# Prompt attention of a hybrid decoder layer: triangular sums in two fp32r passes instead of one fp32 product

## The reference

```
z = einsum('bqhd,bkhd->bhqk', q, k) * HEAD_DIM ** -0.5 + bias
mask = kpos[None, :] < qpos[:, None]
log_1m = where(mask, log_sigmoid(-z), 0.0)
between = cumsum(log_1m, axis=3, reverse=True) - log_1m
weights = exp(where(mask, log_sigmoid(z) + between, -inf))
out = einsum('bhqk,bkhd->bqhd', weights, v)
```

## Time and profile before

| | |
|---|---|
| median of 3 runs | 2051.55 us |
| the profiled execution | 2058.1 us, its span 2056.5 us |
| TensorE busy in the span | 1851.8 us (90%), 13899 matmuls |
| VectorE, ScalarE, GpSimd busy | 820.1, 614.7, 397.1 us |
| prompt attention | from 392.2 to 510.9 us of the span |
| decode, linear attention, RWKV | behind it, to about 1100 us |
| output projection and MLP | the rest |

### The profile page before, as it was taken

One profiled execution on the slowest core, in us unless ns is written; L12 is line 12 of the kernel. 1 busy time (PEld: TensorE's weight loads), 2 busy tenths in 40 slices (PEclk: granted clock), 3 DMA queues, 4 the chain that ended last, 5 costly groups with the idle time before them and its releaser, 6 DMA issues.

```text
span 2056.5 us, 33982 instructions
## 1 busy us (share of the span) xinstructions
PE 1851.8 (90%) x13899; PEld 1539.0 (75%) x13899; DVE 820.1 (40%) x1286; ACT 614.7 (30%) x1421; POOL 397.1 (19%) x606
## 2 busy tenths in 40 slices
PE   4999999999766798688886996999999999999996
PEld 4999999843435675577784445988888888999995
DVE  7111111265437673533321445333344333433336
ACT  3111111365546555322221222222222222222223
POOL 6400021487353556100010001000000000000004
PEclk9999999999777655697877998999999999999998
DMA  5111121200541011000003201111111111111102
GB/s 152 52 42 40 44 90 55 80 7 2 178 133 35 26 31 28 1 2 1 2 1 124 62 26 51 41 41 41 41 41 54 48 41 41 41 50 52 41 20 87
DMA packets 103829, 100.07 MB, mean 49 GB/s; under 512 B 15522, under 2 KB 89906, under 8 KB 103714
## 3 DMA queue, kind: packets, MB, share of 16 engines
q1 hardware_dynamic: 91266, 81.15, 13.2%
q0 software_dynamic: 6720, 17.11, 2.7%
q10 hardware_dynamic: 5728, 0.19, 0.2%
HBM read 85.78 MB, written 12.65 MB: 48 GB/s over the span
## 4 chain that ended last, share of the span: by engine, by line
PE 51%; DVE 4%; ACT 1%; DMA 1%; issue 1%; POOLq 0%; POOL 0%; SPq 0%; DVEq 0%
PE ps L416 12%; PE ps L417 12%; PE ps L418 12%; PE ps L2407 6%; PE ps L2052 1%; PE ps L1978 1%; DVE arena L2161 1%; DVE arena L2566 1%; PE ps L2073 1%; PE ps L2069 1%; DMA arena<-in_w_out 1%; PE ps L2105 1%; PE ps L2094 1%; PE ps L2125 0%; PE ps L2123 0%
## 5 line engine op out<-in xcount | busy, mean ns | idle before, releaser
L416 PE MATMUL ps<-h_split,w_split 128*128 128x384 f32 (+1 forms) x768 | 251.1, 327 | 3.4 <-DVE w_split L2550 3.4
L418 PE MATMUL ps<-h_split,w_split 128*128 128x384 f32 (+1 forms) x768 | 250.9, 327 | 0.0
L417 PE MATMUL ps<-h_split,w_split 128*128 128x384 f32 (+1 forms) x768 | 250.9, 327 | 0.0
L2577 DVE TENSOR_TENSOR arena<-arena,ps 128x1024 f32<-128x1024 f32 x144 | 175.5, 1219 | 164.3 <-PE ps L418 164.3
L417 PE MATMUL ps<-w_split,u_split 128*128 128x512 f32 (+1 forms) x576 | 224.5, 390 | 0.0
L416 PE MATMUL ps<-w_split,u_split 128*128 128x512 f32 (+1 forms) x576 | 224.4, 390 | 0.0
L418 PE MATMUL ps<-w_split,u_split 128*128 128x512 f32 (+1 forms) x576 | 224.3, 389 | 0.0
L2599 POOL TENSOR_TENSOR arena<-arena 128x1024 f32<-128x1024 f32 (+1 forms) x9 | 23.3, 2594 | 773.7 <-DVE arena L2566 773.7
L2558 DVE TENSOR_TENSOR u_split<-above_u_split,u_split 128x384 fp32r<-128x384 f32 (+1 forms) x96 | 51.5, 537 | 297.2 <-ACT above_u_split L2531 297.1
L2510 ACT ACTIVATE w_split<-below_w_split 128x1024 fp32r<-128x1024 f32 x64 | 64.1, 1048 | 339.1 <-PE ps L418 321.7
L416 PEld LDWEIGHTS ps<-h_split,w_split 128*128 128x128 f32 x768 | 144.7, 188 | 5.1 <-issue 3.6
(11 more groups left out here) (380 smaller groups left out, 3532.4 us busy)
## 6 DMA issues: line engine op xcount, KB each, us to landing
below_w_split<-in_w_up SPq DMA_DIRECT2D x32, 512.0 KB, 4.9
below_w_split<-in_w_down SPq DMA_DIRECT2D x32, 512.0 KB, 3.8
w_raw<-in_w_in SPq DMA_DIRECT2D x27, 512.0 KB, 3.9
arena<-in_x_prompt SPq DMA_DIRECT2D x16, 512.0 KB, 3.7
arena<-in_cache_sb_k SPq DMA_DIRECT2D x64, 128.0 KB, 2.4
arena<-in_cache_sb_v POOLq DMA_DIRECT2D x64, 128.0 KB, 2.6
nat_scratch<-nat_stage POOLq DMA_DIRECT2D x32, 128.0 KB, 2.0
arena<-nat_scratch SPq DMA_DIRECT2D x16, 256.0 KB, 2.7
```

Of the source, the lines that this page charges most:

```text
L416: pe.matmul(out, w_hi, x_hi, start=first, stop=False)
L417: pe.matmul(out, w_hi, x_lo, start=False, stop=False)
L418: return pe.matmul(out, w_lo, x_hi, start=False, stop=last)
L2577: dve.tensor_tensor(y_acc[0:r, i, :], y_acc[0:r, i, :], p, ALU.add).then_inc(S("dn_out"), 1)
```

## The change

The triangular product of `exponents` is done in two fp32r passes over a high and a low part of the softplus. The triangle is copied to an fp32r tile (`sb_tri`) once. For each block ScalarE copies the softplus of both heads to `sb_hi` with rounding to fp32r (`high`), and VectorE subtracts that from the softplus into `sb_lo` (`low`); both tiles have one buffer, so `high(n)` waits for `exponents(n - 1)`. The mask product uses bf16 copies of `ident` and `neg_big`. The sum product stays fp32. VectorE's order becomes low(n + 1), clipped(n + 3), softplus(n + 2); in ScalarE's, high(n + 1) stands between weights(n) and log_sums(n + 2). `exponents` waits for `sb_sum` and `sb_lo` at the head of the products that need them.

```
+        sb_eye, sb_mask = (mixT[:, n, T:TOK].bitcast(BF16) for n in range(2))
...
             def exponents(n):
                 pe.wait_ge(S("sb_sp"), n + 1)
-                if kt < 4 * G + 3:
-                    pe.wait_ge(S("sb_sum"), n)
-                if kt >= 4 * G:
-                    pe.wait_ge(S("sb_spm"), sb_diagonals(n))
                 for c in range(2):
                     bank = ps[:, 2 * (n % 3) + c, 0:w]
                     if kt >= 4 * G:
-                        pe.matmul(bank[:, 0:P], ident, neg_big, start=False, stop=False, skip_group_check=True)
+                        pe.matmul(bank[:, 0:P], sb_eye, sb_mask, start=False, stop=False, skip_group_check=True)
                     if kt < 4 * G + 3:
+                        if c == 0:
+                            pe.wait_ge(S("sb_sum"), n)
                         pe.matmul(bank, neg_ones, sb_sum[:, (n - 1) % 2, c, c0:512], ...)
-                    pe.matmul(bank, neg_tri, sb_sp[:, n % 3, c, 0:w], start=False, stop=True,
-                              skip_group_check=True).then_inc(S("sb_x"), 1)
+                    if c == 0:
+                        pe.wait_ge(S("sb_lo"), n + 1)
+                    pe.matmul(bank, sb_tri[:, :], sb_hi[:, c, 0:w], start=False, stop=False, skip_group_check=True)
+                    pe.matmul(bank, sb_tri[:, :], sb_lo[:, c, 0:w], start=False, stop=True, skip_group_check=True)\
+                        .then_inc(S("sb_x"), 1)
...
+            def low(n):
+                w = sb_geometry(n)[4]
+                dve.wait_ge(S("sb_hi"), n + 1)
+                dve.tensor_tensor(sb_lo[:, :, 0:w], sb_sp[:, n % 3, :, 0:w], sb_hi[:, :, 0:w].bitcast(F32),
+                                  ALU.subtract).then_inc(S("sb_lo"), 1)
+
             clipped(0)
+            dve.tensor_copy(sb_tri[:, :], neg_tri).then_inc(*did("dve"))
+            dve.tensor_copy(sb_eye, ident).then_inc(*did("dve"))
+            dve.tensor_copy(sb_mask, neg_big).then_inc(*did("dve"))
+            dve.wait_ge(*so_far("dve"))
             clipped(1)
+            softplus(dve, 0)
+            clipped(2)
+            softplus(dve, 1)
+            low(0)
             for n in range(SBN):
-                softplus(dve, n)
+                if n + 1 < SBN:
+                    low(n + 1)
+                if n + 3 < SBN:
+                    clipped(n + 3)
                 if n + 2 < SBN:
-                    clipped(n + 2)
+                    softplus(dve, n + 2)
...
             if n >= 3:
-                dve.wait_ge(S("sb_x"), 2 * (n - 2))
                 dve.wait_ge(S("sb_sum"), n - 2)
...
+            def high(n):
+                act.wait_ge(S("sb_sp"), n + 1)
+                if kt >= 4 * G:
+                    act.wait_ge(S("sb_spm"), sb_diagonals(n))
+                if n >= 1:
+                    act.wait_ge(S("sb_x"), 2 * n)
+                act.activation(sb_hi[:, :, 0:w], sb_sp[:, n % 3, :, 0:w], ACT.Copy).then_inc(S("sb_hi"), 1)
+
             log_sums(0)
             log_sums(1)
+            high(0)
             for n in range(SBN):
                 weights(n)
+                if n + 1 < SBN:
+                    high(n + 1)
                 if n + 2 < SBN:
                     log_sums(n + 2)
```

More of the change, by code:

```diff
@@ L572, in build @@
         sb_sum = at(WR + 3072, 2, 2, 512)
+        with ExitStack() as place:
+            place.enter_context(nc.sbuf_tensor("below_sb_hi", [P, CONST_END + 2 * TOK], F32))
+            sb_hi = place.enter_context(nc.sbuf_tensor("sb_hi", [P, 2, 512], F32R))
+            place.enter_context(nc.sbuf_tensor("below_sb_lo", [P, TOK - 1024], F32))
+            sb_lo = place.enter_context(nc.sbuf_tensor("sb_lo", [P, 2, 512], F32R))
+            place.enter_context(nc.sbuf_tensor("below_sb_tri", [P, WR + 5120 - CONST_END - 3 * TOK - 1024], F32))
+            sb_tri = place.enter_context(nc.sbuf_tensor("sb_tri", [P, P], F32R))
+        sb_eye, sb_mask = (mixT[:, n, T:TOK].bitcast(BF16) for n in range(2))
         def sb_geometry(n):
@@ L705, in log_sums @@
                 act.activation(zc, zc, ACT.Ln, bias=one_col).then_inc(S("sb_l"), 1)
+            def high(n):
+                pr, G, kt, q0, w, c0, hg = sb_geometry(n)
+                act.wait_ge(S("sb_sp"), n + 1)
[4 more added lines that the diff above has]
+                act.activation(sb_hi[:, :, 0:w], sb_sp[:, n % 3, :, 0:w], ACT.Copy).then_inc(S("sb_hi"), 1)
             log_sums(0)
             log_sums(1)
+            high(0)
             for n in range(SBN):
                 weights(n)
+                if n + 1 < SBN:
+                    high(n + 1)
                 if n + 2 < SBN:
```

## The result

The changed kernel takes 2079.14 us in the median of 4 runs (2076.9 to 2085.8) beside 2055.47 for the kernel before (4 runs). The ratio is 1.0112, with a 95% interval of 1.0083 to 1.0142: slower by about 23 us. The profiled execution has a span of 2075.9 us.

What follows compares the result with a forecast made beforehand. TensorE's issue bounds the stage before; afterwards the 18.7 us saved stay hidden behind VectorE and GpSimd. The median 2051.6, plus 20.5 for the loop and head and 5 for the clock, gives 2077 us; range 2056 to 2095.

Steps and rivals of the forecast that it cites:

- TensorE's issue was the bound before: In prompt attention before the change, TensorE issues without idle time, so its 5.70 us per full-width block is the period.
- the port: In prompt attention, a VectorE operation with two SBUF inputs waits until GpSimd's current one is over; L674 takes 1.30 median.
- `low` waits out a sum and then needs 1.1 us: In each full block, low waits out GpSimd's 2.36 us sum, then needs 1.1: 3.7 us from softplus to its end.
- E(3): E(n) is the end of exponents(n), where outputs starts; E(3) to E(7) was forecast at 21.5 us against 18.3.
- VectorE goes ahead of GpSimd's next operation: Where GpSimd has its next operation ready, the waiting two-input VectorE operation goes first, as the row at 467.04 shows.
- The periods: From low(n) to low(n+1): 6.4 us in full blocks off the diagonal against 5.70, and 6.8 in 512-wide diagonal ones.
- The head of the stage: Before E(3): low(0) lies behind copies and other VectorE work, +2.8 us, and the three blocks to E(3) lose about 0.9.
- the three copies: At the stage's start, three VectorE copies of 128 columns before low(0): 0.6 us together, at most 1.3.
- The clock: TensorE's waits in the stage lower its clock: two to three falls at about 2 us, +5; upper bound +60.
- The gross saving of 18.7 us: On TensorE in the stage: 13.7 us from the fp32r triangular products and 5.0 from bf16 mask products, if TensorE stays the bound.
- TensorE busy for 95 to 105 us in the stage: A sign to look for in the changed kernel's trace, in a prompt attention stage of about 140 us.
- The rival that `low` does not wait: In the stage, low does not wait for the port: plain period 5.1 us, total 2051, or 2036 if VectorE hides; 8%.

Runs made afterwards that it cites:

- the short shift: The changed kernel with only GpSimd's token-shift operations cut to 72 or fewer columns, sums at full size: 2079.13 us (one run).
- the swapped order: The changed kernel with VectorE's order low(n+1), softplus(n+2), clipped(n+3), so softplus before clipped: 2076.5 us (4 runs), ratio to the kernel before 1.0098.
- GpSimd's operations short: The changed kernel with sums cut to 8 columns per head and token-shift operations to 72 or fewer, waits kept: 2055.35 us (10 runs), ratio 0.9998.

## Why the prediction was right, point by point

- **TensorE's issue was the bound before: right, but for a few diagonal blocks.** The bf16 mask alone shortens the stage, only where masks are, and in eight of twelve diagonal blocks by the whole saving. In three blocks TensorE already waited for the port, 1.3 us together.
- **`low` waits out a sum and then needs 1.1 us: right, and nearly the whole cause.** It ends 1.08 behind the sum in each plain block, and with no long operation on GpSimd 21.2 of the 22.8 us are gone; the head keeps 3.9 of its 5.6, against a gain of 2.3 behind E(3).
- **VectorE goes ahead of GpSimd's next operation: right**, though it rested on one row; a shift behind a sum now lasts 2.5 to 3.4 us in each block where `low` falls into the sum, against 2.0 to 2.4 before. The Trainium skill, "SBUF — State Buffer", section "Summary: rules for kernel authors", says that with two SBUF inputs on VectorE and a GpSimd operation that reads SBUF, the second one to issue is blocked fully until the first finishes. The trace agrees: `low` ends 1.08 us behind the sum, about what its 1024 columns take by themselves (1.23 us for the whole operation with the port free).
- **The periods: right within 3% by group, in part by luck.** Plain 6.2 against 6.4. Group by group, forecast and measured: E(3) to E(7) 21.5 and 21.7, E(7) to E(11) 24.8 and 24.3, E(11) to E(23) 67.3 and 68.0. Single diagonal blocks miss by more and in both directions: those 384 wide were forecast at 6.0 and took 6.68, 7.55 and 5.28, those 512 wide at 7.2 and took 6.64, 5.94 and 7.73. The forecast periods hold no loss of clock and the measured ones do, as the point on the clock shows.
- **The head of the stage: too cheap.** From first scores to E(3) I forecast 3.7 more; it is 25.5 against 19.9, 5.6 more. The step that failed is the three copies "0.6 together, at most 1.3": they took 1.7. The first two waited for GpSimd's clearing, 393.14 to 394.96, as VectorE's and GpSimd's timelines of the changed kernel show:

```profile
393.50 1.54 DVE L669 CAST sb_tri<-arena 128x128 fp32r<-128x128 f32 x1
393.63 1.48 DVE L670 CAST arena<-arena 128x128 bf16<-128x128 f32 x1
395.03 0.21 DVE L671 CAST arena<-arena 128x128 bf16<-128x128 f32 x1
```

```profile
393.14 1.82 POOL L762 MEMSET arena<- 128x2048 f32 x1
```

 The rest of the 1.9 fits a lower clock at the head. With the short shift the head goes the same way up to the end of `low` of block 1, 10.8 us behind the first scores in both runs; from there to E(1) it takes 2.65 us at a granted clock of 0.70 instead of 3.54 at 0.50, which is 0.9 less.
- **The clock: about the right size, and inside the loop.** I added 5 us for two to three falls. Rows of the changed kernel's TensorE windows, in plain blocks and in diagonal ones:

```profile
440.00:444.00 4.00, 2.93 (x12) 1.00 0.00 0
444.00:448.00 4.00, 4.00 (x15) 1.00 0.01 4
474.00:478.00 4.00, 2.59 (x6) 0.50 0.00 0
478.00:482.00 4.00, 4.00 (x13) 0.50 0.00 0
```

 Behind E(3) the granted clock fell to 0.50, that is to 1.2 GHz, four times, in the products of blocks 6, 14, 17 and 19, all diagonal. Blocks 14 and 18 are both 384 wide; here, from the timeline of the changed kernel, are `low` and E of block 14 with the sum behind it, then `low` and E of block 18:

```profile
474.74 1.89 DVE L665 TENSOR_TENSOR sb_lo<-arena,sb_hi 128x768 fp32r<-128x768 f32 x1 [0.96 <-ACT sb_hi L739]
479.78 1.12 PE L633 MATMUL ps<-arena 128*64 128x256 f32 x4
480.11 2.35 POOL L771 TENSOR_TENSOR arena<-arena 128x1024 f32<-128x1024 f32 x1 [1.61 <-PE ps L621]
...
496.61 1.89 DVE L665 TENSOR_TENSOR sb_lo<-arena,sb_hi 128x768 fp32r<-128x768 f32 x1 [0.96 <-ACT sb_hi L739]
500.23 0.65 PE L633 MATMUL ps<-arena 128*64 128x256 f32 x4
```

 From the end of `low` to E it takes 3.15 us in block 14, at 0.50, and 1.73 in block 18, at 1.00. The next sum and the next `high` start from E(14), so the 1.4 us are lost to the loop. Read in the same way against a block of the same width at 1.00, blocks 6, 17 and 19 lose 0.55, 0.84 and 0.53: an estimate of 3.3 us behind E(3), beside the 0.9 at the head. The forecast of the loop alone, 113.6 us from E(3) to E(23), meets the measured 114.0 only because its own terms were about 2.9 too dear. In the plain blocks of this run, with a wait of 1.0 us each, the clock stayed at 1.00; in the runs with the swapped order and with the short shift it fell in plain blocks too.
- **The gross saving of 18.7 us: a little too high.** A plain block's own work on TensorE is 5.03, so 0.67 is saved there and not 0.8. It stayed hidden, so the sum did not feel it.
- **TensorE busy for 95 to 105 us in the stage: wrong**, 110, at a mean granted clock of 0.89. With GpSimd's operations short, and 0.97 in its stage, it is 100, so the lower clock accounts for the excess as far as these two runs tell.
- **The rival that `low` does not wait** would have given 2051. Freed of the port, the kernel took 2055 with a stage 1.6 longer than before: the rival's price was right to a few microseconds, its condition did not hold.

Part of the closeness is luck. For the stage 25.5 us were forecast: 16.8 for the loop behind E(3), 3.7 for the head and 5 for the clock. Measured are 22.8: 17.2 behind E(3), of which some 3.3 are the clock, and 5.6 at the head. So the loop's own terms were 2.9 too dear and the head 1.9 too cheap, and these offset each other. The total was also put on a median of the kernel before of 2051.55, which is 3.9 lower than in the runs compared here.

## What to carry to other kernels

Before an operation with two SBUF inputs is given to VectorE, look at what GpSimd does in those microseconds: the price is not its own duration but the rest of GpSimd's operation in flight, and if both start from the same event, the greater part of that operation. Then write down each loop from one block to the next with such waits in it; shortening the one that binds only shows the next (here VectorE with GpSimd, then GpSimd with TensorE, then TensorE alone). A wait put into TensorE's work can cost twice: here the clock fell in four of the blocks that waited, and the slower products stood in the same loop. A cheaper product saves only what its feeding chain does not take back.

## What was not expected of the hardware

Two VectorE operations met GpSimd's clearing of SBUF, which only writes, and fared differently. The copies of one input waited for it to the end (1.54 and 1.48 us instead of the 0.21 of the third, above). The two-input subtraction ran through the middle of one at its usual price; GpSimd's and VectorE's timelines of the changed kernel:

```profile
418.03 1.80 POOL L762 MEMSET arena<- 128x2048 f32 x1
```

```profile
418.97 0.43 DVE L665 TENSOR_TENSOR sb_lo<-arena,sb_hi 128x256 fp32r<-128x256 f32 x1 [1.16 <-ACT sb_hi L739]
```

The Trainium skill, "SBUF — State Buffer", section "Who interferes with whom", states both halves: copies may run in a mode that takes the shared pair of ports whole, while a second input takes only its reading side and so meets only operations of GpSimd that read. The trace agrees in both: 1.54 us against 0.21 for copies, and 0.43 for the subtraction inside the clearing.
